# FFN gate and up products by Strassen's scheme for two of eight k-pairs, in a float32 kernel of split matmuls

## The chip, the cores and the metric

One core of a Trainium2 chip. The metric is the device time of one execution in microseconds; the kernel before was run three times. TensorE is the matmul engine, VectorE (DVE) and ScalarE (ACT) do elementwise work, GpSimd (POOL) and SyncE (SP) issue DMAs here.

## What is computed

Two layers on x of 256 tokens by 2048, all in float32. The first is a hybrid attention layer, the second a FFN, a mixer and another FFN. The change touches the two FFNs alone:

```python
def rmsnorm(x, g): ...
def swiglu(x, w_gate, w_up, w_down):
    return (jax.nn.silu(x @ w_gate) * (x @ w_up)) @ w_down
```

x is 256 x 2048, w_gate and w_up are 2048 x 5632, w_down is 5632 x 2048. The result is added, times 0.5, to the residual.

## The kernel before, in words

**Split products.** TensorE works on fp32r operands. To keep float32 accuracy each operand is split into a rounded part and the rest: weights into whi and wlo, activations into act_hi and act_lo. A product is three matmuls: hi x whi, lo x whi, hi x wlo. The fourth is left out.

**Groups and units.** Weights stream from HBM in groups of TILES = 2 blocks of 128 rows (a k-pair) by W = 512 columns, 512 KB. A ring of RING = 4 places holds raw, whi and wlo. Of each group SyncE loads raw (`load`, L388; waits until wlo of the group four before is done, lo_ready), ScalarE rounds it to whi (`split_hi`, L1036; waits for the load and for group_used of the group four before), VectorE subtracts to get wlo (`split_lo`, L1496), and TensorE does 2 tiles x 2 token halves x 3 = 12 matmuls of 128x128 by 512 (`groups`, L573; all of one tile kind before the next, so wlo is waited for just before the last four). ScalarE and VectorE run AHEAD = 3 groups ahead of TensorE. A unit is all k-pairs (G_D = 8) of one block of 512 columns and fills one PSUM pair acc (two token halves).

**The FFN loop.** For each of FF_CHUNKS = 11 column blocks there is a gate unit and an up unit. The first block is written out, the other 10 are turns of a hardware loop (`at.loop`) on each engine; `ffn` in TensorE's, ScalarE's, VectorE's and SyncE's programs (L917, L2090, L407). At the end of the gate unit ScalarE puts the silu of acc times the row scale in g_sb (`activate`, L1171). At the end of the up unit VectorE forms h_sb (`gated`, L2114: two scalar_tensor_tensor from PSUM, then a transpose of 32x32 squares into h_turned). GpSimd then exchanges the squares through DRAM (`exchange`, L482: one DMA out, a wait, four DMAs back into h_back), and in the next turn at j == 5 ScalarE (`turned_hi`, L1114) and VectorE (`turned_lo`, L1570) write h_hi and h_lo from h_back. Each engine works strictly in the order written, so whatever stands behind these waits for them.

**Semaphores.** `Place` (L154) counts groups, units and so on, and turns the counts into targets of waits inside loops. `raw_in` has one semaphore for each ring place, `lo_ready`, `hi_ready` and `group_used` count groups, `acc_free` the halves of a PSUM pair that were read. The PSUM banks tr0, tr1, s_ps and o_ps are used in attention and not in the FFN loop.

Of the kernel before, what the change touches and what calls it, by code (L numbers as in the profile page):

```python
# [24 lines left out]
F32 = mybir.dt.float32  # L25
F32R = mybir.dt.float32r
I32 = mybir.dt.int32
ACT = mybir.ActivationFunctionType
# [4 lines left out]
P = 128  # L33
D = 2048
SEQ = 256
# [55 lines left out]
ALL_GROUPS = (FIRST_GROUPS + CHUNKS * G_D + 2 * (FF_CHUNKS * 2 * G_D + CHUNKS * KF // TILES)  # L91
              + 15 * G_D + CHUNKS * (2 * G_D + 2 + 6) + CHUNKS * G_D)

# [57 lines left out]
    return n  # L151


class Place:  # L154

    def __init__(self):
        self.n = dict(group=0, unit=0, job=0, chunk=0, ready=0, score=0, value=0, turn=0)  # L160
        self.turn, self.adds = None, {}

    def target(self, what, more=0, times=1, ring=1):
# [19 lines left out]
def build(nc, x, positions, w_in, w_uq, w_ukv, b_forget, w_out, g_post, ffn1_w_gate_2, ffn1_w_up_2,  # L183
# [3 lines left out]
    with ctx:  # L187
# [80 lines left out]
        h_turned, h_back = top, top + QUADS * TURN * 4  # L268
        h_turned, _ = place_at("h_turned", [P, CHUNK], F32, h_turned)
        h_back, _ = place_at("h_back", [P, CHUNK], F32, h_back)  # L270
        gfinal, top = place_at("gfinal", [P, D], F32, top)


        sg_hi, top = place_at("sg_hi", [P, SG_GROUPS, SEQ], F32R, region)
# [94 lines left out]
        vector_step = sem("vector_step")  # L369
        pool_step = sem("pool_step")  # L370
        out_a, out_v, out_sent = sem("out_a"), sem("out_v"), sem("out_sent")

        block = ctx.enter_context(nc.Block())


        after_first = FIRST_GROUPS + CHUNKS * G_D
        after_ffn1 = after_first + FF_CHUNKS * 2 * G_D + CHUNKS * KF // TILES
# [7 lines left out]
        def _(sp):  # L385
# [19 lines left out]
                at.n["unit"] += 1  # L405

            def ffn(w_gate, w_up, w_down):  # L407
                for i in at.loop(sp, FF_CHUNKS, dict(group=2 * G_D, unit=2)):
                    unit(w_gate, G_D, i * W)
                    unit(w_up, G_D, i * W)  # L410
                for c in range(CHUNKS):
                    unit(w_down, KF // TILES, c * W)

# [155 lines left out]
        def _(pe):  # L569
# [3 lines left out]
            def groups(count, hi, lo, width=W, opening_from=None, between=None, ends_by_half=0):  # L573
# [73 lines left out]
                at.n["unit"] += 1  # L647

            def job(blocks):

# [266 lines left out]
            def ffn(first_one):  # L917
                chunks_split[0] = at.n["chunk"]

                def second_half():  # L920

                    pe.wait_ge(post_part, 2)
                    for part in range(2):
                        transpose_part(1, part)
                    at.n["chunk"] += 1
                    at.n["ready"] += 1
                    keep_warm(2)

                for j in groups(G_D, act_hi, act_lo, opening_from=POST_OPENED if first_one else None,
                                between=second_half):  # L930
                    if first_one:
                        if j in (0, 2, 4):
                            opening(j // 2 + 1)
                    if not first_one and j == 3:
                        exchanged()
                        chunk_is_split()
                        transpose_chunk(xres, 3 * W)
                    if not first_one and j == 5:
                        chunk_is_split()
                for j in groups(G_D, act_hi, act_lo):  # L940
                    pass
                for i in at.loop(pe, FF_CHUNKS - 1, dict(group=2 * G_D, unit=2, chunk=1)):
                    for j in groups(G_D, act_hi, act_lo):
                        if j == 3:
                            h_turns()
                    for j in groups(G_D, act_hi, act_lo):
                        pass
# [83 lines left out]
        def _(act):  # L1031
# [4 lines left out]
            def split_hi(n):  # L1036
# [10 lines left out]
                if m >= RING:  # L1047

                    act.wait_ge(group_used, at.target("group", n + 1 - RING))
                nc.scalar.activation(whi[:, slot, :, 0:width], raw[:, slot, :, 0:width],  # L1050
                                     ACT.Copy).then_inc(hi_ready, 1)

            def groups(count, last_split=True):
                for j in range(count):
                    if last_split or j < count - 1:
                        split_hi(AHEAD)
                    at.n["group"] += 1
                    yield j
                at.n["unit"] += 1

            def unit_ready():

# [278 lines left out]
            def ffn(norm, first_one):  # L1341
# [12 lines left out]
                        norm_ready(norm)  # L1354
                        activate(g_sb, ACT.Silu, norm)
                for j in groups(G_D):
                    pass
                at.n["turn"] = EX_FFN1 if first_one else EX_FFN2
                for i in at.loop(act, FF_CHUNKS - 1, dict(group=2 * G_D, unit=2, chunk=1, turn=1)):
                    for j in groups(G_D):  # L1360
                        if j == 5:
                            turned_hi(h_hi, i * 4, h_back[:])
                        if j == 7:
                            activate(g_sb, ACT.Silu, norm)
                    for j in groups(G_D):
                        pass
# [119 lines left out]
        def _(dve):  # L1486
# [9 lines left out]
            def split_lo(n):  # L1496

                m = at.n["group"] + n
                if at.turn is None and m >= ALL_GROUPS:
                    return  # L1500
                width = LAT2 if LAT2_FIRST <= m < LAT2_END else W
                slot = m % RING
                dve.wait_ge(hi_ready, at.target("group", n + 1))
                nc.vector.tensor_tensor(wlo[:, slot, :, 0:width], raw[:, slot, :, 0:width],  # L1504
                                        whi[:, slot, :, 0:width].bitcast(F32), ALU.subtract).then_inc(lo_ready, 1)

            def groups(count, last_split=True):
                for j in range(count):
# [581 lines left out]
            def ffn(norm, first_one):  # L2090
# [23 lines left out]
                def gated():  # L2114
# [6 lines left out]
                    for half in range(HALVES):  # L2121
# [5 lines left out]
                                        h_sb[:].rearrange("p h (k q j) -> p (h k) q j", q=QUADS, j=QUAD)  # L2127
                                        ).then_inc(turned, 1)

                for j in groups(G_D):  # L2130
                    if j == 7:
                        gated()
                at.n["turn"] = EX_FFN1 if first_one else EX_FFN2
                for i in at.loop(dve, FF_CHUNKS - 1, dict(group=2 * G_D, unit=2, chunk=1, chunk_job=2, turn=1)):
                    for j in groups(G_D):
                        if j == 5:
                            turned_lo(h_hi, h_lo, i * 4, h_back[:])
                    for j in groups(G_D):
                        if j == 7:
                            gated()  # L2140
# [284 lines left out]
```

## Time and profile before

| what | value |
|---|---|
| device time, three runs | 2606.83, 2606.23, 2605.05 us; median 2606.23 |
| profiled execution: span, first to last instruction | 2603.4 us |
| its own time | not listed apart; one of the runs above, 1.7 to 3.4 us over the span |
| TensorE, matmuls | busy 2594.2 us, 11669 matmuls |
| VectorE | busy 1503.5 us (58%) |
| ScalarE | busy 1191.6 us (46%) |
| mean DMA rate | 216 GB/s |

The span is what the trace covers. Busy matmul time counts overlapping matmuls once; the mean of one matmul (391 ns) includes its overlap with its neighbours, so the spacing of matmuls is read from the timeline.

### The profile page before, as it was taken

The numbers are of one execution on the slowest core, as the hardware profiler recorded it, in microseconds if no ns is written. First come the engines' busy times: TensorE is split into PE (matmuls) and PEld (weight loads), VectorE is DVE, ScalarE is ACT, GpSimd is POOL, SyncE is SP. The second block draws the span as 40 slices with busy tenths as digits, with TensorE's granted clock in tenths as the row PEclk, the third lists the DMA queues.
The fourth block names the chain that finished last, engine by engine and source line by source line (L and its number), as shares of the span: only waits on it lengthen the run. The fifth ranks groups of instructions, "written<-read, shape, count | busy, mean of one in ns | idle before, by whom it ended". The sixth has DMA issues, their size and how long they took to land.

```text
span 2603.4 us, 31908 instructions
## 1 busy us (share of the span) xinstructions
PE 2594.2 (100%) x11669; PEld 2154.1 (83%) x11669; DVE 1503.5 (58%) x1725; ACT 1191.6 (46%) x1362; POOL 204.5 (8%) x345
## 2 busy tenths in 40 slices
PE   9999999999999999999999999999999999999998
PEld 8888888888888888888888888888888888888887
DVE  7766665755555555556555765555655555555554
ACT  5544554544444444444444644444454444444333
POOL 0122110000000000001100420000000000000000
PEclk9999999999999999999999999999999999999999
DMA  7787785677777766668876677665777777777564
GB/s 217 255 255 233 217 242 182 206 209 225 209 225 209 226 209 209 210 210 258 241 216 193 199 224 216 210 209 193 236 209 217 217 216 217 214 219 228 193 194 157
DMA packets 280065, 561.51 MB, mean 216 GB/s; under 512 B 22826, under 2 KB 25784, under 8 KB 279720
## 3 DMA queue, kind: packets, MB, share of 16 engines
q1 hardware_dynamic: 257120, 489.61, 62.0%
q0 software_dynamic: 22208, 70.19, 9.1%
q8 instruction: 56, 0.92, 0.1%
q10 hardware_dynamic: 648, 0.52, 0.1%
q14 instruction: 33, 0.27, 0.0%
HBM read 526.02 MB, written 34.22 MB: 215 GB/s over the span
## 4 chain that ended last, share of the span: by engine, by line
PE 99%; DMA 0%; ACT 0%; SPq 0%; issue 0%; DVE 0%; ACTq 0%
PE acc L586 97%; PE s_ps L740 1%; PE o_ps L764 1%; PE tr L656 1%; DMA xres<-in_x 0%; PE tr L991 0%; ACT xres L1477 0%; ACT g_sb L1145 0%; ACT act_hi L1094 0%; DVE xres L1782 0%; SPq L396 0%; SPq L417 0%; SPq L415 0%; ACT root L1152 0%; PE s_ps L869 0%
## 5 line engine op out<-in xcount | busy, mean ns | idle before, releaser
L1504 DVE TENSOR_TENSOR wlo<-raw,whi 128x1024 fp32r<-128x1024 f32 x929 | 1130.5, 1224 | 982.0 <-ACT whi L1050 977.2
L1050 ACT ACTIVATE whi<-raw 128x1024 fp32r<-128x1024 f32 x929 | 977.8, 1057 | 1148.7 <-PE acc L586 1115.2
L586 PE MATMUL acc<-whi,act_hi 128*128 128x512 f32 (+1 forms) x2560 | 690.5, 391 | 0.1
L586 PE MATMUL acc<-whi,act_lo 128*128 128x512 f32 (+1 forms) x2560 | 683.3, 388 | 0.0
L586 PE MATMUL acc<-wlo,act_hi 128*128 128x512 f32 (+1 forms) x2560 | 683.1, 388 | 0.0
L586 PEld LDWEIGHTS acc<-whi,act_lo 128*128 128x128 f32 x2560 | 479.4, 188 | 100.2 <-DVEq L1545 0.4
L586 PEld LDWEIGHTS acc<-wlo,act_hi 128*128 128x128 f32 x2560 | 479.5, 188 | 99.9 <-DVE wlo L1504 0.3
L586 PEld LDWEIGHTS acc<-whi,act_hi 128*128 128x128 f32 x2560 | 474.9, 188 | 94.8 <-issue 0.3
L586 PE MATMUL acc<-whi,h_hi 128*128 128x512 f32 x704 | 188.8, 389 | 0.0
L586 PE MATMUL acc<-wlo,h_hi 128*128 128x512 f32 x704 | 188.8, 389 | 0.0
L586 PE MATMUL acc<-whi,h_lo 128*128 128x512 f32 x704 | 188.8, 389 | 0.0
L586 PEld LDWEIGHTS acc<-whi,h_lo 128*128 128x128 f32 x704 | 132.1, 188 | 27.5
L586 PEld LDWEIGHTS acc<-wlo,h_hi 128*128 128x128 f32 x704 | 132.1, 188 | 27.4
L586 PEld LDWEIGHTS acc<-whi,h_hi 128*128 128x128 f32 x704 | 132.1, 188 | 27.4
L485 POOL DMA_DIRECT2D turn_dram<-h_turned x25 | 14.0, 561 | 1110.4 <-DVE h_turned L2126 947.5
L499 POOL DMA_DIRECT2D h_back<-turn_dram x100 | 54.7, 554 | 76.4 <-DMA turn_dram<-h_turned 73.7
L1176 ACT ACTIVATE g_sb<-acc,rs 128x512 f32<-128x512 f32 x44 | 27.9, 686 | 33.2 <-PE acc L586 33.2
L1194 ACT ACTIVATE lat<-lat,soft 128x128 f32<-128x128 f32 (+1 forms) x32 | 14.3, 448 | 61.8 <-DVE soft L1734 61.8
L2122 DVE SCALAR_TENSOR_TENSOR h_sb<-acc,rs,g_sb 128x512 f32<-128x512 f32 x44 | 31.0, 746 | 12.0 <-PE acc L586 12.0
L586 PE MATMUL acc<-whi,o_hi 128*128 128x512 f32 x128 | 35.3, 392 | 0.0
L586 PE MATMUL acc<-whi,o_lo 128*128 128x512 f32 x128 | 34.9, 389 | 0.0
L586 PE MATMUL acc<-wlo,o_hi 128*128 128x512 f32 x128 | 34.9, 389 | 0.0
(281 smaller groups left out, 1372.8 us busy)
## 6 DMA issues: line engine op xcount, KB each, us to landing
raw<-in_w_in SPq DMA_DIRECT2D x280, 512.0 KB, 4.5
raw<-in_ffn_w_gate SPq DMA_DIRECT2D x176, 512.0 KB, 4.4
raw<-in_ffn_w_up SPq DMA_DIRECT2D x176, 512.0 KB, 4.1
raw<-in_ffn_w_down SPq DMA_DIRECT2D x176, 512.0 KB, 4.6
raw<-in_w_out SPq DMA_DIRECT2D x64, 512.0 KB, 4.7
turn_dram<-h_turned POOLq DMA_DIRECT2D x25, 512.0 KB, 3.2
h_back<-turn_dram POOLq DMA_DIRECT2D x100, 128.0 KB, 5.6
raw<-in_w_sg_out SPq DMA_DIRECT2D x24, 512.0 KB, 4.2
```

The lines of the kernel that those rows point to most:

```text
L485: pool.dma_start(turn_dram[n % 2][:, :, 0:run], left.rearrange("p (q r) -> p q r", q=QUADS)).then_inc(turn_left, 16)
L499: pool.dma_start(back[quad * QUAD:(quad + 1) * QUAD].rearrange("p (a r) -> p a r", a=QUADS), blocks[n % 2][quad][:, :, 0:run]).then_inc(tu ...
L586: return nc.tensor.matmul(pair[:, half, 0:width], left[:, j * TILES + t, half * P:(half + 1) * P], right[:, (first_group + j) % RING, t, 0 ...
L656: last = nc.tensor.transpose(tr[bank][0:rows, cols], src, ident[0:src.shape[0], 0:src.shape[0]])
L740: last = nc.tensor.matmul(out_cols, left, right, start=(n == 0), stop=(n == len(terms) - 1), skip_group_check=True)
L764: last = nc.tensor.matmul(o_ps[:, qb * P:(qb + 1) * P], left, right, start=(n == 0), stop=(n == len(terms) - 1), skip_group_check=True)
L1050: nc.scalar.activation(whi[:, slot, :, 0:width], raw[:, slot, :, 0:width], ACT.Copy).then_inc(hi_ready, 1)
L1176: last = nc.scalar.activation(dest[:, half, :], a[:, half, :], func, scale=scaled(norm, half))
L1194: last = nc.scalar.activation(src_of[qb], src_of[qb], ACT.Exp, bias=soft[:, 1, qb:qb + 1], scale=scale, accum_out=soft[:, 2, qb:qb + 1])
L1504: nc.vector.tensor_tensor(wlo[:, slot, :, 0:width], raw[:, slot, :, 0:width], whi[:, slot, :, 0:width].bitcast(F32), ALU.subtract).then_in ...
L2122: last = nc.vector.scalar_tensor_tensor(h_sb[:, half, :], a[:, half, :], scaled(norm, half), g_sb[:, half, :], ALU.mult, ALU.mult)
```

## The change

In the 10 loop turns of each FFN, gate and up are computed together in 20 groups. k-pairs 2 to 7 are done as before, gate ("left") and up ("right"). k-pairs 0 and 1 are each a product of 2x2 blocks: token halves by two k tiles, times two k tiles by gate and up. Strassen's scheme gives its four results from seven block products in place of eight, each still three matmuls. Such a k-pair takes four groups. "four_left" is the loaded gate tiles, "four_right" the loaded up tiles (only the second is split and multiplied), "outer" and "inner" are sums of weight tiles, which VectorE writes into the next two ring places of raw (`outer_sums`, `inner_sums`) and which are then split like loaded ones. The four sums of activations are formed once for each FFN (`combine_activations`) in the first block's up unit, and rounded by ScalarE. The extra products go to the four free banks; VectorE recombines them (`fours_out`) at group 13 and adds acc at the end of the turn (`paired_gated`). The silu runs on g_sb in SBUF after that. SyncE's first block is now written out too. Cut to its core:

```diff
+FOURS = 2
+CHUNK_ORDER = ([("left", k) for k in range(2, 6)] + four(0) + [("left", 6), ("left", 7)] + four(1)
+               + [("right", k) for k in range(2, G_D)])
+q1, q5, q6, q7 = s_ps, o_ps, tr[0], tr[1]
...
 SyncE, ffn
-                for i in at.loop(sp, FF_CHUNKS, dict(group=2 * G_D, unit=2)):
+                unit(w_gate, G_D, 0)
+                unit(w_up, G_D, 0)
+                for i in at.loop(sp, FF_CHUNKS - 1, dict(group=CHUNK_GROUPS, unit=2)):
+                    for kind, k in CHUNK_ORDER:
+                        if kind in ("left", "four_left"):
+                            load(w_gate, k, i * W + W)
+                        elif kind in ("right", "four_right"):
+                            load(w_up, k, i * W + W)
+                        else:
+                            at.n["group"] += 1
...
 TensorE, paired: what each kind of group multiplies (bank, left hi, left lo, tile)
+                    if kind == "four_left":
+                        return [block(q1[:], 0, 2 * k, 0), block(left[:, 0, :], 0, 2 * k + 1, 1)]
+                    if kind == "four_right":
+                        return [combined(right[:, 0, :], k, 0, 1)]
+                    if kind == "outer":
+                        t1 = outer_tiles(m - 2)[1]
+                        return [combined(q5[:], k, 1, t1), combined(q7[:], k, 3, 1 - t1)]
+                    return [combined(q6[:], k, 2, 0), block(left[:, 1, :], 1, 2 * k + 1, 1)]
...
 ScalarE, loop turn
+                    for j in paired():
                         if j == 5:
                             turned_hi(h_hi, i * 4, h_back[:])
+                        if j == LAST_FOUR:
+                            unit_ready()
+                            nc.scalar.activation(g_sb[:, 0, :], q1[:], ACT.Copy).then_inc(q1_copied, 1)
+                        if j == LAST_FOUR + 2:
+                            act.wait_ge(acc_free[at.n["unit"] % 2], at.target("unit", 0, 2, 2) + 2)
...
 VectorE, split_lo and the sums
+                if sums_next:
+                    outer_sums(m + 1)
                 dve.wait_ge(hi_ready, at.target("group", n + 1))
...
+                if sums_next:
+                    inner_sums(m + 1)
+            def outer_sums(m):
+                raw_filled(m)
+                raw_filled(m + 1)
+                dve.wait_ge(lo_ready, at.target("group", m - 1 - at.n["group"]))
+                slot = (m + 2) % RING
+                nc.vector.tensor_tensor(raw[:, slot, :, :], raw_blocks[:, outer_tiles(m)[0], :],
+                                        raw[:, (m + 1) % RING, 0, :].unsqueeze(1).to_broadcast([P, TILES, W]),
+                                        ALU.add).then_inc(raw_in[slot], 16)
+            def inner_sums(m):
+                raw_filled(m + 2)
+                dve.wait_ge(lo_ready, at.target("group", m - at.n["group"]))
+                slot = (m + 3) % RING
+                nc.vector.tensor_tensor(raw[:, slot, 0, :], raw[:, (m + 2) % RING, outer_tiles(m)[1], :],
+                                        raw[:, (m + 1) % RING, 1, :], ALU.add).then_inc(sum_step, 1)
+                dve.wait_ge(sum_step, at.target("sums"))
+                nc.vector.tensor_tensor(raw[:, slot, 1, :], raw[:, slot, 0, :], raw[:, m % RING, 1, :],
+                                        ALU.add).then_inc(raw_in[slot], 16)
+            def fours_out():
+                unit_ready()
+                dve.wait_ge(q1_copied, at.target("paired", 1))
+                sum_settled(nc.vector.tensor_tensor(h_sb[:, 1, :], q6[:], g_sb[:, 0, :], ALU.add))
+                sum_settled(nc.vector.tensor_tensor(g_sb[:, 1, :], q7[:], h_sb[:, 1, :], ALU.add))
+                sum_settled(nc.vector.tensor_tensor(h_sb[:, 0, :], q5[:], h_sb[:, 1, :], ALU.subtract))
+                sum_settled(nc.vector.tensor_tensor(h_sb[:, 1, :], q5[:], g_sb[:, 1, :], ALU.subtract))
+                dve.sem_inc(q_free, 1)
+                nc.vector.tensor_tensor(g_sb[:], acc[at.n["unit"] % 2][:], g_sb[:],
+                                        ALU.add).then_inc(acc_free[at.n["unit"] % 2], 2)
...
 VectorE, end of a turn
+                def paired_gated():
+                    unit_ready()
+                    right = (at.n["unit"] + 1) % 2
+                    for half in range(HALVES):
+                        nc.vector.tensor_tensor(h_sb[:, half, :], acc[right][:, half, :], h_sb[:, half, :],
+                                                ALU.add).then_inc(acc_free[right], 1)
+                    dve.wait_ge(acc_free[right], at.target("unit", 1, 2, 2) + 2)
+                    dve.wait_ge(gate_ready, at.target("paired", 1))
...
+                        if j == LAST_FOUR:
+                            fours_out()
+                        if j == CHUNK_GROUPS - 1:
+                            paired_gated()
```

`LAST_FOUR` is 13. `outer_tiles` picks the two tiles of gate and up that an outer sum adds to. `combine_activations` is one sum of 1024 columns, four of 256, a wait for ScalarE's rounding, and one difference; it runs at j == 1, the rounding at j == 2.

## Rows read from the trace of the kernel before

**Rows 1.** The page: engine totals, granted clock by slices, chain that ended last.
```profile
PE 2594.2 (100%) x11669; PEld 2154.1 (83%) x11669; DVE 1503.5 (58%) x1725; ACT 1191.6 (46%) x1362; POOL 204.5 (8%) x345
...
PEclk9999999999999999999999999999999999999999
...
PE 99%; DMA 0%; ACT 0%; SPq 0%; issue 0%; DVE 0%; ACTq 0%
```
**Rows 2.** Busy time by engine, 506.9 to 942 us; waits there: total, times, longest.
```profile
core 0: us, PE busy (x) PEld busy (x) DVE busy (x) ACT busy (x) POOL busy (x), PEclk, DMA share, GB/s
506.90:942.00 435.10, 435.10 (x1921) 360.29 (x1920) 232.93 (x211) 192.01 (x200) 27.51 (x50) 1.00 0.73 217
...
ACT whi L1050 <- PE acc L586: 222.0, 145, 1.7
DVE wlo L1504 <- ACT whi L1050: 194.2, 135, 2.6
```
**Rows 3.** Timeline of a turn: start, duration, engine, line; in brackets idle before.
```profile
894.20 1.07 PE L586 MATMUL acc<-whi,act_hi 128*128 128x512 f32 x4
894.55 1.41 DVE L2122 SCALAR_TENSOR_TENSOR h_sb<-acc,rs,g_sb 128x512 f32<-128x512 f32 x2 [0.56 <-PE acc L586]
896.00 1.25 DVE L2126 STREAM_TRANSPOSE h_turned<-h_sb 128x1024 f32<-128x1024 f32 x1
897.16 2.32 DVE L1504 TENSOR_TENSOR wlo<-raw,whi 128x1024 fp32r<-128x1024 f32 x2
899.63 1.07 PE L586 MATMUL acc<-whi,act_hi 128*128 128x512 f32 x4
899.84 1.06 ACT L1050 ACTIVATE whi<-raw 128x1024 fp32r<-128x1024 f32 x1 [1.66 <-PE acc L586]
900.93 1.23 DVE L1504 TENSOR_TENSOR wlo<-raw,whi 128x1024 fp32r<-128x1024 f32 x1 [1.45 <-ACT whi L1050]
901.01 2.19 POOL L499 DMA_DIRECT2D h_back<-turn_dram  x4 [2.91 <-DMA turn_dram<-h_turned]
902.36 1.07 PE L586 MATMUL acc<-whi,act_hi 128*128 128x512 f32 x4
...
909.96 1.16 ACT L1122 ACTIVATE h_hi<-h_back 128x512 f32 x2 [0.90 <-DMA h_back<-turn_dram]
...
938.07 1.41 DVE L2122 SCALAR_TENSOR_TENSOR h_sb<-acc,rs,g_sb 128x512 f32<-128x512 f32 x2 [0.56 <-PE acc L586]
```
**Rows 4.** Timeline of TensorE at the kernel's end, twelve matmuls running to one bank.
```profile
2585.14 0.62 PE L586 MATMUL acc<-whi,h_hi 128*128 128x512 f32 x2
...
2587.86 0.62 PE L586 MATMUL acc<-whi,h_hi 128*128 128x512 f32 x2
```
**Rows 5.** Groups of instructions by form: count, busy us, mean ns, idle before.
```profile
L2087 DVE TENSOR_TENSOR xres<-xres,gfinal 128x512 f32<-128x512 f32 x6 | 3.9, 688 | 0.2
L2321 DVE TENSOR_TENSOR ln_gb<-ln_gb 128x1024 f32<-128x1024 f32 x4 | 4.9, 1225 | 0.1
L1581 DVE TENSOR_TENSOR h_lo<-h_back,h_hi 128x512 f32 x40 | 25.8, 687 | 6.7 <-ACT h_hi L1122 6.6
L1122 ACT ACTIVATE h_hi<-h_back 128x512 f32 x40 | 23.0, 623 | 13.5 <-DMA h_back<-turn_dram 13.5
L1176 ACT ACTIVATE g_sb<-acc,rs 128x512 f32<-128x512 f32 x44 | 27.9, 686 | 33.2 <-PE acc L586 33.2
```
**Rows 6.** DMA issues, six successive 2.72 us stretches from 899.07; us to landing.
```profile
raw<-in_ffn_w_up SPq DMA_DIRECT2D x1, 512.0 KB, 6.3
raw<-in_ffn_w_up SPq DMA_DIRECT2D x1, 512.0 KB, 7.0
raw<-in_ffn_w_up SPq DMA_DIRECT2D x1, 512.0 KB, 5.9
raw<-in_ffn_w_up SPq DMA_DIRECT2D x1, 512.0 KB, 4.4
raw<-in_ffn_w_up SPq DMA_DIRECT2D x1, 512.0 KB, 3.5
raw<-in_ffn_w_up SPq DMA_DIRECT2D x1, 512.0 KB, 3.6
```
**Rows 7.** Timeline of GpSimd in the second FFN, one exchange's way back.
```profile
2059.22 1.10 POOL L499 DMA_DIRECT2D h_back<-turn_dram  x2 [3.17 <-DMA turn_dram<-h_turned]
2062.82 1.10 POOL L499 DMA_DIRECT2D h_back<-turn_dram  x2 [2.51 <-issue]
```
**Rows 8.** The tile raw: who waited for its loads (us, times).
```profile
  ACT whi L1050: 32.2, 19
```

More of the change, by code:

```diff
@@ L151, in raw_target, with outer_tiles @@
     return n
+def outer_tiles(m):
+    left, right = m % RING, (m + 1) % RING
+    blocks = (TILES * left, TILES * right + 1)
+    if blocks[0] < blocks[1]:
+        return slice(blocks[0], blocks[1] + 1, blocks[1] - blocks[0]), 0
+    return slice(blocks[1], blocks[0] + 1, blocks[0] - blocks[1]), 1
 class Place:
     def __init__(self):
-        self.n = dict(group=0, unit=0, job=0, chunk=0, ready=0, score=0, value=0, turn=0)
+        self.n = dict(group=0, unit=0, job=0, chunk=0, ready=0, score=0, value=0, turn=0, paired=0, sums=0)
         self.turn, self.adds = None, {}
@@ L270, in build @@
         h_back, _ = place_at("h_back", [P, CHUNK], F32, h_back)
+        four_hi, four_lo = (h[:, KF - 4 * FOURS // TILES:KF, :].rearrange("p k n -> p (k n)").rearrange(
+            "p (q i n) -> p q i n", q=FOURS, i=4) for h in (h_hi, h_lo))
         gfinal, top = place_at("gfinal", [P, D], F32, top)
+        four_raw = h_turned[:].rearrange("p (q i n) -> p q i n", q=FOURS, i=4)
+        four_x = h_sb[:].rearrange("p h n -> p (h n)").rearrange("p (k n) -> p k n", n=SEQ)
         sg_hi, top = place_at("sg_hi", [P, SG_GROUPS, SEQ], F32R, region)
@@ L941, in ffn @@
                     pass
-                for i in at.loop(pe, FF_CHUNKS - 1, dict(group=2 * G_D, unit=2, chunk=1)):
-                    for j in groups(G_D, act_hi, act_lo):
+                pe.wait_ge(four_ready, 1 if first_one else 2)
+                for i in at.loop(pe, FF_CHUNKS - 1, dict(group=CHUNK_GROUPS, unit=2, chunk=1, paired=1)):
+                    for j in paired(act_hi, act_lo):
                         if j == 3:
                             h_turns()
-                    for j in groups(G_D, act_hi, act_lo):
-                        pass
                 for c in range(CHUNKS):
@@ L1049, in split_hi @@
                     act.wait_ge(group_used, at.target("group", n + 1 - RING))
-                nc.scalar.activation(whi[:, slot, :, 0:width], raw[:, slot, :, 0:width],
+                tiles = slice(1, 2) if KIND.get(m) == "four_right" else slice(0, TILES)
+                nc.scalar.activation(whi[:, slot, tiles, 0:width], raw[:, slot, tiles, 0:width],
                                      ACT.Copy).then_inc(hi_ready, 1)
@@ L1059, in groups, with paired @@
                 at.n["unit"] += 1
+            def paired():
+                for j in range(CHUNK_GROUPS):
+                    split_hi(AHEAD)
+                    at.n["group"] += 1
+                    yield j
+                at.n["unit"] += 2
+                at.n["paired"] += 1
             def unit_ready():
@@ L1502, in split_lo @@
                 slot = m % RING
+                sums_next = KIND.get(m + 1) == "four_left"
+                if sums_next:
+                    outer_sums(m + 1)
+                tiles = slice(1, 2) if KIND.get(m) == "four_right" else slice(0, TILES)
                 dve.wait_ge(hi_ready, at.target("group", n + 1))
-                nc.vector.tensor_tensor(wlo[:, slot, :, 0:width], raw[:, slot, :, 0:width],
-                                        whi[:, slot, :, 0:width].bitcast(F32), ALU.subtract).then_inc(lo_ready, 1)
+                nc.vector.tensor_tensor(wlo[:, slot, tiles, 0:width], raw[:, slot, tiles, 0:width],
+                                        whi[:, slot, tiles, 0:width].bitcast(F32), ALU.subtract).then_inc(lo_ready, 1)
@@ new lines, in split_lo, with raw_filled @@
+                if sums_next:
+                    inner_sums(m + 1)
+            raw_blocks = raw[:].rearrange("p s t n -> p (s t) n")
+            def raw_filled(m):
+                target = raw_target(m)
+                if at.turn is not None:
+                    target = target + at.turn * (16 * at.adds["group"] // RING)
+                dve.wait_ge(raw_in[m % RING], target)
+            def outer_sums(m):
[6 more added lines that the diff above has]
+                                        ALU.add).then_inc(raw_in[slot], 16)
@@ L2133, in ffn @@
                 at.n["turn"] = EX_FFN1 if first_one else EX_FFN2
-                for i in at.loop(dve, FF_CHUNKS - 1, dict(group=2 * G_D, unit=2, chunk=1, chunk_job=2, turn=1)):
-                    for j in groups(G_D):
+                for i in at.loop(dve, FF_CHUNKS - 1, dict(group=CHUNK_GROUPS, unit=2, chunk=1, chunk_job=2, turn=1,
+                                                          paired=1, sums=SUMS_PER_CHUNK)):
+                    for j in paired():
                         if j == 5:
                             turned_lo(h_hi, h_lo, i * 4, h_back[:])
-                    for j in groups(G_D):
-                        if j == 7:
-                            gated()
+                        if j == LAST_FOUR:
+                            fours_out()
+                        if j == CHUNK_GROUPS - 1:
+                            paired_gated()
                 next_gain = GAINS["mix"]
```

124 lines of the change are left out of this document (111 added, 13 removed).

## The prediction

> **What bounds the kernel now.** I read the page's engine totals first [rows 1]: TensorE is busy for all of the span and holds 99% of the chain that ended last, at a granted clock of 0.9 or more in every slice. Then one stretch with ten turns of the FFN loop [rows 2]: TensorE has no gap, at clock 1.00, while VectorE is busy for 233 of 435 us and ScalarE for 192. The waits [rows 2] show both standing before a split of the next weights until matmuls are done: 222 us of ScalarE for TensorE, 194 us of VectorE for ScalarE. So the time is the number of matmuls times their spacing, as long as nobody is late. The timeline [rows 3] gives the spacing: twelve matmuls of a group start at 899.63, the next twelve at 902.36, 2.72 us, or 0.2267 us each; the turn is 43.52 us (gated product at 894.55 and at 938.07) for 192 matmuls.
>
> **What a group costs its feeders.** By the same rows, whi starts 0.21 us after TensorE has left the group four places back and takes 1.06; wlo follows 0.03 later and takes 1.23; then its slot of raw is reloaded. The lead is three groups of 2.72 us, and wlo is wanted only for the last third of its own group. That lead hides everything now.
>
> **What goes.** Two k-pairs of each turn need 2 x 21 matmuls, not 2 x 24: 186 per turn, and 6 x 0.2267 = 1.36 us less. Over 2 x 10 turns that is 27.2 us. The order of the banks differs (four_right sends three matmuls running to one bank); at the kernel's end twelve matmuls to one bank take 2587.86 - 2585.14 = 2.72 us [rows 4], so this costs nothing. If nothing were late: 2606.2 - 27.2 = 2579.
>
> **What comes.** In a turn of 20 groups (0 to 19; time 0 is TensorE's start of group 0) the fours are 4 to 7 and 10 to 13. TensorE needs 4.76 us for a four, where four ring places used to last 10.88, and two of the four places hold sums that VectorE writes. Durations [rows 5]: a sum of 1024 columns 1.23, of 512 0.69, a copy of 512 from PSUM 0.69, turned halves on ScalarE 1.15 for two. Two VectorE instructions with no wait between them take 2.32, so the second starts 0.10 before the first ends [rows 3]; one that waits for its predecessor I put 0.03 after it, like wlo after whi. The Trainium skill (VectorE: DVE Perf Modes, section "The DRAIN you can't avoid") says that the next instruction starts only when the pipe has emptied and that leaving out semaphores saves nothing; rows 3 disagree by that 0.10, and by the page the sum below would be some 16 us higher, 2657.
>
> I follow one turn (E3 is the end of group 3; undisturbed ends 10.88, 12.24, 12.92, 14.28, 15.64, then 18.36 and so on).
> (a) VectorE, end of the turn before. The product is formed at 0.36, as now (894.55 - 894.20 [rows 3]), but it first adds acc to the recombined halves (two of 512, 1.30), then multiplies (1.41) and turns (1.25): ready at 4.38, not 3.05, so the exchange leaves 1.33 later. Then sum outer(4) to 5.51, wlo 3 to 6.64, the two inner sums to 8.08, wlo 4 to 9.21, wlo 5 to 9.80, wlo 6 to 10.93. All are in time for TensorE. whi 7 waits for E3: 10.88 + 0.21 + 1.06 = 12.15, so wlo 7 ends at 13.41.
> (b) SyncE loads 8, 9, 10, 11 behind wlo 4, 5, 6, 7: issued at 9.38, 9.97, 11.10, 13.58, no longer 2.72 apart. They fall on the exchange's way back, issued from about 8.1 on (4.38 + 901.01 - 897.25). Loads issued beside that now land after 6.3, 7.0, 5.9 and 4.4 us, later ones after 3.5 to 3.6 [rows 6]. By their distance from it I take 6.3, 6.2, 5.6, 4.6 (estimates between these rows): landed 15.68, 16.17, 16.70, 18.18. Bounds: 3.6 each, and 7.0, 7.0, 6.3, 5.4.
> (c) whi 8 ends at 16.79, TensorE starts 8 at 16.82, not 15.64: **1.18 lost**. h_back lands 12.7 after the turning (909.96 - 897.25 [rows 3]), at 17.1; ScalarE, which has whi 9 queued behind turned_hi, ends the latter at 18.2 and whi 9 at 19.3, VectorE ends h_lo at 18.9. TensorE is at 8 until 19.54.
> (d) Behind h_lo VectorE does outer(10), which needs load 11, to 20.3, wlo 9 to 21.47 (wanted 21.35, **0.15 lost**), the inner sums to 22.9, wlo 10 to 24.04 (TensorE at 10 from 22.41, wants it at 23.3: **0.76 lost**). wlo 11 to 13 are in time; E13 = 27.92.
> (e) Load 14 goes only behind wlo 10: 24.2 + 3.6 = 27.8, whi 14 ends 28.92, **1.03 lost** before group 14.
> (f) fours_out at group 13 (q1 copy, four sums with waits, one of 1024: 4.9 us) delays wlo 17 to 37.6, wanted at 38.9; nothing lost. The silu on SBUF is on nobody's way; with fours_out gone later by over 1.3 us group 17 would wait.
> Sum: 3.1 lost - 1.36 gained = **+1.75 us a turn**, a turn of 45.27; times 20, +35.0. Against this execution's span 2603.4 that is 2638.4, and on the median shown, which is 2.8 above the span: **2641**.
> Hidden: combining activations once per FFN (VectorE about 5 us, ScalarE 1.06) in the second unit of the first turn, where wlo 5 slips to about 4.8 us after E1 and is wanted at 10; its cover is that unit's idle VectorE, and without it the price were under 10 us in all. Peeling SyncE's first turn, zero. The later exchange before the down projection meets groups of 2.72 with a lead of over 7 us at that place, zero; ends: 0 and the 1.33 of its delay, twice.
>
> **Rivals.**
> 1. *The lead hides it all.* For it: feeders half idle now [rows 2]. Against: their idleness is spread over 2.72 us groups, and (d) and (e) have two loads in series. 2579. Chance 0.08.
> 2. *The loads land undisturbed.* With no load in flight between groups 0 and 4 the exchange may come back about 1 us earlier and all loads take 3.6: then (c) goes, (d) and (e) stay in part; the turn is 44.05, +11. In the best corner, the exchange never waited for, 43.39: -3. So 2617, and down to 2603. Chance 0.22. It turns to a gain only if outer(10) runs before 17.2 and group 14 loses under 1.36 in sum.
> 3. *Forecast*, chance 0.46.
> 4. *Worse contention.* Loads at their upper bounds, exchange back after 13.4, load 14 after 4.4: turn 46.77, +65, 2671. For it: loads now go in bunches, and one exchange already had its four reads split by 2.51 us of standing [rows 7]. Chance 0.20.
> 5. *The clock falls.* For 14 of 20 turns or so one 12-matmul group at half clock (2.72 more) would give +38 on top, about 2680. Against: [rows 1] show no lower slice, and my gaps are near 1 us. The Trainium skill (TensorE: Matmul & The Clock Gate, section "HAM oscillation — how this bites in real kernels") says that a TensorE waiting for data between short bursts can be throttled each time; no row here shows it. Chance 0.04.
> That the change would not remove matmuls is excluded by the diff: 21 for 24 is written out.
>
> **How the numbers follow.** 0.2%, about what a measurement of this kernel can tell, is 5.2 us. Faster: rival 1 and the best corner of 2 (0.05): 0.13. Same: a part of 2 (0.07). Slower: the rest of 2 (0.10), 3, 4, 5: 0.80. The range leaves out rival 1, most of 5 and the tail of 4: 2600 to 2674.
>
> **What would show it.** In the profile of after: MATMUL counts lower by 120; turns of 45.3 us between turnings; ScalarE's whi waiting for DMA raw in about two places a turn (now 19 times in the whole kernel [rows 8]); TensorE gaps of about 1 us before groups 8 and 14, each 20 times, and before the wlo products of group 10; h_back landing near 17 us after the turn's start with ScalarE behind it. It is wrong if TensorE keeps no gap, if gaps stand at group 4 or 17 instead (VectorE's own work), or if loads 8 to 11 land in under 4 us.

## The result, and the profile after

The changed kernel takes **2670.24 us** (median of 4 runs, 2666.60 to 2673.38) against 2606.53 us before (4 runs beside it, 2605.05 to 2610.46): ratio 1.0244, 95% interval 1.0229 to 1.0258, so 63.7 us slower. The sign and the range of the forecast hold; its size, +35, does not. The profiled execution of after is the fastest of the four: own time 2666.6 us, span 2664.8, mean granted clock 0.996 (before 0.999). Its span is 61.4 us longer than the 2603.4 of the profiled execution of before.

Totals and chain on the page of after, to be held against [rows 1]:
```profile
span 2664.8 us, 32709 instructions
PE 2597.6 (97%) x11549; PEld 2132.5 (80%) x11549; DVE 1769.4 (66%) x2077; ACT 1259.4 (47%) x1464; POOL 202.7 (8%) x345
PE 54%; issue 22%; DMA 11%; DVE 9%; ACT 2%; POOL 1%; DVEq 0%; ACTq 0%; SPq 0%; POOLq 0%
raw<-in_ffn_w_gate SPq DMA_DIRECT2D x176, 512.0 KB, 5.2
raw<-in_ffn_w_up SPq DMA_DIRECT2D x176, 512.0 KB, 4.6
h_back<-turn_dram POOLq DMA_DIRECT2D x100, 128.0 KB, 2.9
```
TensorE held 99% of the chain; now it holds 54%, DMA has 11% and VectorE 9%, and 22% is "issue", time in which the profile shows nothing that the engine waited for. TensorE is idle for 67 us (2664.8 - 2597.6), 57 of them in the two stretches of gate and up. Who waited there (total us, times, longest):
```profile
ACT whi L1164 <- DMA raw<-in_ffn_w_gate: 156.8, 83, 4.7
ACT whi L1164 <- DMA raw<-in_ffn_w_up: 92.6, 70, 3.8
PE acc L747 <- ACT whi L1164: 44.4, 38, 4.6
PE s_ps L754 <- DVE wlo L1637: 9.2, 15, 0.6
PE acc L754 <- DVE wlo L1637: 3.2, 13, 0.4
ACT h_hi L1244 <- DMA h_back<-turn_dram: 15.0, 3, 5.5
```
ScalarE waited 19 times for a load of raw in the whole kernel before [rows 8]; now 153 times for loads of gate and up alone. One turn (group 0 starts at 733.36), timeline of after: start, duration, engine, line, in brackets the idle before. It answers to [rows 3].
```profile
733.77 1.22 DVE L1637 TENSOR_TENSOR wlo<-raw,whi 128x1024 fp32r<-128x1024 f32 x1 [1.22 <-ACT whi L1164]
734.92 1.28 DVE L2346 TENSOR_TENSOR h_sb<-acc,h_sb 128x512 f32<-128x512 f32 x2
737.68 1.25 DVE L2354 STREAM_TRANSPOSE h_turned<-h_sb 128x1024 f32<-128x1024 f32 x1
...
742.39 2.19 POOL L548 DMA_DIRECT2D h_back<-turn_dram  x4 [2.61 <-DMA turn_dram<-h_turned]
742.68 4.09 DVE L1637 TENSOR_TENSOR wlo<-raw,whi 128x1024 fp32r<-128x1024 f32 x4
744.07 2.11 SPq L437 DMA_DIRECT2D raw<-in_ffn_w_gate  x3
...
749.58 1.06 ACT L1164 ACTIVATE whi<-raw 128x1024 fp32r<-128x1024 f32 x1 [4.08 <-DMA raw<-in_ffn_w_gate]
750.55 1.14 ACT L1244 ACTIVATE h_hi<-h_back 128x512 f32 x2
750.69 1.20 PE L747 MATMUL acc<-whi,act_hi 128*128 128x512 f32 x4 [1.53 <-ACT whi L1164]
751.81 1.29 DVE L1792 TENSOR_TENSOR h_lo<-h_back,h_hi 128x512 f32 x2
753.33 1.23 DVE L1657 TENSOR_TENSOR raw<-raw 128x1024 f32<-128x1024 f32 x1 [0.23 <-issue]
755.75 1.20 PE L754 MATMUL acc<-wlo,act_hi 128*128 128x512 f32 x4 [0.22 <-DVE wlo L1637]
758.47 0.50 PE L754 MATMUL s_ps<-wlo,act_hi 128*128 128x512 f32 x1 [0.61 <-DVE wlo L1637]
762.04 1.06 ACT L1164 ACTIVATE whi<-raw 128x1024 fp32r<-128x1024 f32 x1 [3.59 <-DMA raw<-in_ffn_w_up]
763.15 1.20 PE L747 MATMUL acc<-whi,act_hi 128*128 128x512 f32 x4 [0.53 <-ACT whi L1164]
...
783.63 1.25 DVE L2354 STREAM_TRANSPOSE h_turned<-h_sb 128x1024 f32<-128x1024 f32 x1
```
TensorE waits in four places: before group 8 (750.69) for a whi that had waited 4.08 us for load 8; at the wlo products of 9 (755.75) and of 10 (758.47) for VectorE, whose outer sum (753.33) stood behind h_lo until 753.10 and then another 0.23 us for load 11, issued at 746.80 and landed 6.4 us later; and before group 14 (763.15) for a whi that had waited 3.59 us for load 14. The same turn by stretches (stretch, us, busy PE, PEld, DVE, ACT, POOL, then clock, share of the DMA engines, GB/s):
```profile
737.68:747.50 9.82, 9.82 (x45) 8.14 (x44) 8.88 (x9) 2.76 (x3) 2.75 (x5) 1.00 0.44 141
747.50:752.50 5.00, 3.47 (x16) 2.55 (x15) 1.83 (x3) 2.92 (x4) 0.00 (x0) 1.00 0.94 347
752.50:758.50 6.00, 5.17 (x23) 3.62 (x21) 5.57 (x8) 3.72 (x5) 0.00 (x0) 1.00 0.01 3
758.50:772.00 13.50, 12.97 (x56) 10.43 (x57) 10.87 (x12) 6.15 (x7) 0.00 (x0) 1.00 0.81 272
772.00:783.63 11.63, 11.63 (x53) 9.64 (x52) 9.19 (x10) 7.01 (x8) 0.00 (x0) 1.00 0.68 225
```
**Loads come in bunches.** During a four two of the four places of raw hold sums, so SyncE has nothing to load; then all places come free nearly at once. SyncE issues nothing between 732.58 and 744.07. Before, the stretch of ten turns moved 217 GB/s [rows 2], and in one turn of it (720 to 760) pieces of 5 and 10 us moved 144 to 256; now 347 GB/s and a DMA share of 0.94 are followed by 3 GB/s and 0.01. Loads 8 to 11 land after 5.4, 6.1, 6.2 and 6.4 us, in the bunch and beside the exchange.

**The sum closes.** Turns are 46.47 us long on average in the first FFN ((970.56 - 505.87)/10 between turnings) and 47.06 in the second ((2423.06 - 1952.49)/10), before 43.52. Against the undisturbed 42.16 (186 x 0.2267), ten turns of each lose 43.1 + 49.0 = 92.1 us; less the 27.2 that went, that is +64.9 in the loops. The span of this execution grew by 61.4, so the sum closes within 3.5 us, and the rest of the program is that much shorter, most of it (3.2 us) behind the last turning. The 63.7 is the difference of the medians, not of these two executions.

### The profile page after: what moved, and what is told of

It reads as the page before. It is cut to its first block, busy times and chain, and to the rows that moved or that the text cites. A ratio compares the mean times of both kernels' runs of the same rounds, so it can differ in the third digit from the quotient of the medians.

```text
span 2664.8 us, 32709 instructions
## 1 busy us (share of the span) xinstructions
PE 2597.6 (97%) x11549; PEld 2132.5 (80%) x11549; DVE 1769.4 (66%) x2077; ACT 1259.4 (47%) x1464; POOL 202.7 (8%) x345
## 4 chain that ended last, share of the span: by engine, by line
PE 54%; issue 22%; DMA 11%; DVE 9%; ACT 2%; POOL 1%; DVEq 0%; ACTq 0%; SPq 0%; POOLq 0%
PE acc L635 45%; DMA raw<-in_ffn_w_up 7%; DVE wlo L1637 6%; PE acc L747 2%; PE acc L754 2%; PE acc L750 2%; DMA raw<-in_ffn_w_gate 2%; ACT whi L1164 2%; DMA qk<-turn_dram 1%; DMA turn_dram<-turned_s 1%; DVE raw L1667 1%; PE s_ps L854 1%; DVE raw L1657 1%; PE tr L770 1%; DMA turn_dram<-mix_turned 1%
## 5 line engine op out<-in xcount | busy, mean ns | idle before, releaser
L1637 DVE TENSOR_TENSOR wlo<-raw,whi 128x1024 fp32r<-128x1024 f32 (+2 forms) x1009 | 1191.9, 1200 | 763.4 <-ACT whi L1164 756.2
L1164 ACT ACTIVATE whi<-raw 128x1024 fp32r<-128x1024 f32 (+2 forms) x1009 | 1037.4, 1038 | 1113.9 <-PE acc L635 641.2
L635 PE MATMUL acc<-whi,act_hi 128*128 128x512 f32 (+1 forms) x1280 | 348.5, 393 | 0.1
L635 PE MATMUL acc<-whi,act_lo 128*128 128x512 f32 (+1 forms) x1280 | 341.2, 388 | 0.0
L635 PE MATMUL acc<-wlo,act_hi 128*128 128x512 f32 (+1 forms) x1280 | 341.1, 388 | 0.0
L747 PE MATMUL acc<-whi,act_hi 128*128 128x512 f32 x1040 | 294.1, 395 | 44.4 <-ACT whi L1164 44.4
L754 PE MATMUL acc<-wlo,act_hi 128*128 128x512 f32 x1040 | 293.2, 395 | 3.3 <-DVE wlo L1637 3.2
L750 PE MATMUL acc<-whi,act_lo 128*128 128x512 f32 x1040 | 292.3, 394 | 0.0
L635 PEld LDWEIGHTS acc<-wlo,act_hi 128*128 128x128 f32 x1280 | 239.3, 188 | 50.1 <-DVE wlo L1637 0.4
L747 PEld LDWEIGHTS acc<-whi,act_hi 128*128 128x128 f32 x1040 | 192.8, 188 | 99.3 <-ACT whi L1164 60.7
L635 PEld LDWEIGHTS acc<-whi,act_hi 128*128 128x128 f32 x1280 | 234.7, 188 | 44.9 <-issue 0.3
L754 PEld LDWEIGHTS acc<-wlo,act_hi 128*128 128x128 f32 x1040 | 196.2, 190 | 50.7 <-DVE wlo L1637 10.5
```

The costliest lines, as they stand in the source:

```text
L635: return nc.tensor.matmul(pair[:, half, 0:width], left[:, j * TILES + t, half * P:(half + 1) * P], right[:, (first_group + j) % RING, t, 0 ...
L747: nc.tensor.matmul(bank, left_hi, whi[:, slot, t, :], start=fresh, stop=False, skip_group_check=True)
L750: nc.tensor.matmul(bank, left_lo, whi[:, slot, t, :], start=False, stop=False, skip_group_check=True)
L754: last = nc.tensor.matmul(bank, left_hi, wlo[:, slot, t, :], start=False, stop=uses[str(bank)] == o and t == TILES - 1, skip_group_check=True)
L1164: nc.scalar.activation(whi[:, slot, tiles, 0:width], raw[:, slot, tiles, 0:width], ACT.Copy).then_inc(hi_ready, 1)
L1637: nc.vector.tensor_tensor(wlo[:, slot, tiles, 0:width], raw[:, slot, tiles, 0:width], whi[:, slot, tiles, 0:width].bitcast(F32), ALU.subtr ...
```

## The experiments

Every kernel ran beside the kernel before on its chip (2606.2 to 2607.1 us there). Five of them (sums of 16 columns, half loads, both, no recombination, small exchange) leave part of the work out and return other numbers, so they price a part and are no versions to use; the others do all of it. The question: is the loss VectorE's sums, the loads, the recombination, the exchange, or their order?

**Sums of 16 columns.** All instructions, waits and signals stay; the weight sums write only 16 columns.
```diff
-nc.vector.tensor_tensor(raw[:, slot, :, :], raw_blocks[:, outer_tiles(m)[0], :], ...
+nc.vector.tensor_tensor(raw[:, slot, :, 0:16], raw_blocks[:, outer_tiles(m)[0], 0:16], ...
```


> The three weight sums of each four write 16 columns instead of 512 (the rest of those two ring places keeps old data, so the products are of other numbers); all waits stay. Theory A (VectorE's sums stand between the loads that landed and the splits that release the next loads, so the second four runs two loads in series behind them): without 3.7 us of sums per turn of groups 3 to 14 the waits at wlo 9, wlo 10 and before group 14 go and loads 8 to 11 are issued over 2 us earlier; turns near 42.8 us, 2590 to 2602 us in all. Theory B (the loads themselves, bunched because two of four ring places hold sums and slowed by each other, set the time): the bunch only moves, a wait of 1 us or more stays before group 8 or 10, and the time stays above 2630 us.

Measured 2617.79 us (2616.29 to 2619.75), ratio 1.0044 (1.0027 to 1.0061), 52 less than after, and still 39 above the 2579 at which TensorE never waits. What is left, in the waits of this kernel:
```profile
ACT whi L1164 <- DMA raw<-in_ffn_w_up: 83.9, 80, 3.4
ACT whi L1164 <- DMA raw<-in_ffn_w_gate: 79.1, 70, 4.1
```
The result lies between the two theories: without the sums' time, ScalarE still waits 163 us for loads.

**Half loads.** Gate and up loads in the loop bring 256 of 512 columns; all work on them stays.
```diff
+if part is not None:
+    main, cols = part, bass.ds(col, part)
...
-load(w_gate, k, i * W + W)
+load(w_gate, k, i * W + W, part=W // 2)
...
-load(w_up, k, i * W + W)
+load(w_up, k, i * W + W, part=W // 2)
```


> The gate and up loads of the loop turns bring 256 of 512 columns (the rest keeps old data); VectorE, ScalarE and TensorE do the same work. Theory B: landings fall from over 5 us to about 3, the waits before groups 8 and 14 fall by 2 us each turn, time 2610 to 2630 us. Theory A with landings as in the rows of before: the chain of VectorE stays, each of the two loads in series gets at most 1 us shorter, 2635 to 2655 us.

Measured 2590.10 us (2588.62 to 2590.95), ratio 0.9936 (0.9920 to 0.9953), 80 less than after and 20 under the least that either theory gave. Loads (KB, us to landing) and the one wait for sums' work that TensorE keeps:
```profile
raw<-in_ffn_w_gate SPq DMA_DIRECT2D x160, 256.0 KB, 3.2
raw<-in_ffn_w_up SPq DMA_DIRECT2D x160, 256.0 KB, 2.9
PE s_ps L756 <- DVE wlo L1639: 2.8, 10, 0.6
```
With all sums in full, landing 2 us earlier is nearly enough. So loads and sums aren't two losses beside each other but one chain, in which time taken out anywhere counts: 52 + 80 is more than the 91 there is.

**Both.** The two diffs together.

> Sums of 16 columns and loads of 256 columns together (data of other numbers): neither VectorE's sums nor the landings press. The floor of 186 matmuls per turn: 2606.5 less 27.2, 2578 to 2582 us. A time over 2586 would mean that the ring of four places itself costs a short four something, whatever fills it.

Measured 2577.97 us (2577.59 to 2578.59), ratio 0.9888 (0.9871 to 0.9905): the floor. Turnings are 758.73 - 716.57 = 42.16 us apart, 186 x 0.2267 to the hundredth. The matmuls' 27 us are real, and the new order of places and banks costs nothing by itself.

**No recombination.** The four sums of fours_out write 16 columns (the sum with acc stays whole).
```diff
-sum_settled(nc.vector.tensor_tensor(h_sb[:, 1, :], q6[:], g_sb[:, 0, :], ALU.add))
+sum_settled(nc.vector.tensor_tensor(h_sb[:, 1, 0:16], q6[:, 0:16], g_sb[:, 0, 0:16], ALU.add))
```


> The four recombining sums at group 13 work on 16 columns instead of 512 (so h is of other numbers), the sum of 1024 columns stays. Theory C (they hold back wlo 17 and with it the loads of the next turn, so that its wlo 2, the end of turn on VectorE and load 8 come 1.2 us late): the product is formed 0.4 us after the turn's start and not 1.6, the wait before group 8 shrinks from 1.7 to 0.5 us, 20 to 25 us less in all, 2645 to 2652. The prediction's step (f) (nothing lost): 2668 to 2672.

Measured 2645.55 us (2643.45 to 2647.01), ratio 1.0150 (1.0133 to 1.0167), 24.7 less than after. This contradicts step (f) of the prediction. In after fours_out (767.25 to 771.50) holds back the splits, four loads again go out close together and land after 3.5, 4.6, 5.4 and 5.5 us, and wlo 2 of the next turn ends late; the product behind it is formed 1.56 us after that turn's start. Here it is formed 0.20 after it (729.27 against 729.07), and TensorE's gap before group 8, in the same turn, is 0.27 us in place of 1.53.

**Small exchange.** All but the first exchange of each FFN move 16 of 256 columns a run, each way; h_back is otherwise stale.
```diff
+pool.dma_start(turn_dram[n % 2][:, :, 0:16],
+               h_turned[:].rearrange("p (q r) -> p q r", q=QUADS)[:, :, 0:16]).then_inc(turn_left, 16)
```


> From the second block of columns of each FFN on, the exchange moves 16 of 256 columns of each run (the rest of h_back is old data); its DMAs, waits and order stay. If the exchange's way back is what makes load 8 land after 5.4 us (it is issued 1.7 us before that load), the landing falls to about 4.2 and the wait before group 8 from 1.7 to about 0.5 us: 2645 to 2653 us. If the four loads of the bunch slow each other alone, the exchange is harmless and nothing changes: 2665 to 2673.

Measured 2648.43 us (2645.10 to 2650.69), ratio 1.0160 (1.0143 to 1.0177), 21.8 less than after, in the expected range. Its exchange and TensorE's waits:
```profile
h_back<-turn_dram POOLq DMA_DIRECT2D x80, 8.0 KB, 1.9
PE acc L759 <- ACT whi L1176: 17.3, 24, 1.1
PE acc L766 <- DVE wlo L1649: 14.0, 21, 1.1
```
The waits for whi fall from 44.4 to 17.3 us, but part of it only moves on to wlo 9 (14.0): earlier loads meet the same VectorE.

**Turned halves later.** h_back is split at group 9, not 5.
```diff
-                        if j == 5:
+                        if j == 9:
                             turned_hi(h_hi, i * 4, h_back[:])
```


> ScalarE and VectorE take h_back at group 9 of the turn instead of 5. The prediction's steps (c) and (d) put h_hi and h_lo ahead of whi 9 and outer(10); if they are on the path, 0.3 to 0.6 us less per turn, 2655 to 2664 us. If outer(10) waits for load 11 in any case (the profile of after has h_lo ending 0.2 us before that sum starts), nothing: 2666 to 2673.

Measured 2660.22 us (2655.58 to 2661.17), ratio 1.0201 (1.0184 to 1.0218), 10.0 less than after and in the first expected range. But its trace doesn't show that h_lo ahead of outer(10) was what held it. Without h_lo before it, the outer sum waits for load 11 itself (a row of its timeline, one of its waits):
```profile
753.01 1.23 DVE L1657 TENSOR_TENSOR raw<-raw 128x1024 f32<-128x1024 f32 x1 [1.46 <-DMA raw<-in_ffn_w_up]
PE acc L747 <- ACT whi L1164: 24.3, 24, 2.0
```
The gain is in the waits for whi, 24.3 us in all in place of 44.4, in the turn shown 0.94 us before group 8 in place of 1.53. Part of it is lost again in a new wait for wlo of 6.7 us (19 times) in the second four, where the splits of h_back now stand. Why the wait before group 8 shrank was not tried apart.

**The fours further apart.** Three groups between them, not two, and the second four among the up groups.
```diff
-CHUNK_ORDER = ([("left", k) for k in range(2, 6)] + four(0) + [("left", 6), ("left", 7)] + four(1)
-               + [("right", k) for k in range(2, G_D)])
+CHUNK_ORDER = ([("left", k) for k in range(2, 7)] + four(0) + [("left", 7), ("right", 2), ("right", 3)]
+               + four(1) + [("right", k) for k in range(4, G_D)])
```


> Same work, other order: gate pairs 2 to 6, four(0) at groups 5 to 8, gate 7, up 2 and 3, four(1) at 12 to 15, up 4 to 7. With bursts of loads and VectorE's chain together as the cause, one group more ahead of the first four and one more between them take away most of the waits at wlo 9 and 10 and part of the others, but both bursts remain and four(1)'s recombination now ends nearer to the turn's end: 43.0 to 45.0 us per turn, 2596 to 2636 us, middle 2616. If only the number of fours counts and not their distance, 2660 or more.

Measured 2626.29 us (2624.15 to 2627.30), ratio 1.0075 (1.0058 to 1.0092), 43.9 less than after. Nothing was left out: of the 91 us lost, nearly half was the order.

**This order, and h_back at group 10.** The diff above and `j == 10` in place of `j == 5`.

> The spaced order with h_back taken at group 10 instead of 5, so both edits that helped alone. Additive: 2626 less 6 to 10 us, 2616 to 2620. If with the spaced order load 12 and not h_back is what outer waits for: 2624 to 2628.

Measured 2620.86 us (2616.86 to 2622.27), ratio 1.0055 (1.0036 to 1.0073), the best of the complete versions with two fours, and still slower than before. It is 5.4 less than the spaced order alone, just past the additive range (2616 to 2620). TensorE hardly waits for whi any more (17.7 us in the spaced order), and its longest waits are those for wlo inside the fours:
```profile
PE o_ps L754 <- DVE wlo L1637: 11.9, 20, 0.6
PE s_ps L754 <- DVE wlo L1637: 7.7, 15, 0.6
```

**Evenly spread.** The second four at groups 14 to 17 of 20, h_back at 10 (`j == 10` as above).
```diff
+CHUNK_ORDER = ([("left", k) for k in range(2, 6)] + four(0) + [("left", 6), ("left", 7)]
+               + [("right", k) for k in range(2, 6)] + four(1) + [("right", 6), ("right", 7)])
```


> Two fours as far apart as the turn allows: four(0) at groups 4 to 7, gate 6 and 7, up 2 to 5, four(1) at 14 to 17, up 6 and 7; h_back is taken at group 10. Each burst of loads has six whole groups behind it to be made good. If distance is what counts, less is lost than in the spaced order (about 1.9 us per turn): 2600 to 2620 us. Against it: the recombination now starts two groups before the turn's end, and the product and the next turn's sums queue behind it; if that decides, the wait before group 8 is 2 us or more and the time 2630 or more.

Measured 2699.19 us (2698.53 to 2700.92), ratio 1.0354 (1.0336 to 1.0372), the slowest of all. Waits and timeline of this kernel:
```profile
PE acc L747 <- DVE g_sb L1715: 53.8, 18, 3.6
PE acc L747 <- ACT whi L1164: 14.9, 20, 2.7
```
```profile
693.25 2.07 PE L747 MATMUL acc<-whi,act_hi 128*128 128x512 f32 x4 [3.14 <-DVE g_sb L1715]
...
696.61 1.07 PE L754 MATMUL acc<-wlo,act_hi 128*128 128x512 f32 x4
```
The expectation had a late recombination, but not this wait: fours_out alone gives acc of gate back, and with the last four at group 17 the next turn's group 0 waits for it some 3 us, 18 times. At 15 of the 18 the matmuls behind the gap run at half clock (2.07 us for four, not 1.07), and the mean clock is 0.987. The waits for whi did fall, from 44.4 to 14.9 us, but a gap of 3 us in each turn gives the feeders time too, so this run doesn't show that the spreading did it.

**One four.** One of eight k-pairs in place of two, at groups 7 to 10 of 18; two column blocks to a loop turn. Nothing is left out.
```diff
-FOURS = 2
+FOURS = 1
+BLOCKS = 2
...
-CHUNK_ORDER = ([("left", k) for k in range(2, 6)] + four(0) + [("left", 6), ("left", 7)] + four(1)
-               + [("right", k) for k in range(2, G_D)])
+CHUNK_ORDER = ([("left", k) for k in range(1, G_D)] + four(0)
+               + [("right", k) for k in range(1, G_D)])
...
-for i in at.loop(pe, FF_CHUNKS - 1, dict(group=CHUNK_GROUPS, unit=2, chunk=1, paired=1)):
+for i in at.loop(pe, (FF_CHUNKS - 1) // BLOCKS,
+                 dict(group=CHUNK_GROUPS * BLOCKS, unit=2 * BLOCKS, chunk=BLOCKS, paired=BLOCKS)):
+    for b in range(BLOCKS):
```


> One k-pair of eight by seven products instead of two, placed at groups 7 to 10 of 18, after all of gate; the loop takes two blocks of columns per turn so that the ring's places stay fixed. TensorE's work is 13.6 us under before. Theory A and B alike: one four alone is covered by the lead of three groups, since nothing else has to be fed within the next 10 us and the exchange is back before; waits under 0.2 us per block, 2593 to 2598 us, faster than before by 0.3 to 0.5%. If a single four also stalls (about 1.2 us before the group behind it), 2612 to 2620 us.

Measured **2592.20 us** (2591.81 to 2592.91), ratio 0.9943 (0.9926 to 0.9959): 14.9 faster than before and the only complete version here that beats it. Its page (span and totals), and one of its waits:
```profile
span 2591.1 us, 32344 instructions
PE 2580.7 (100%) x11609; PEld 2143.4 (83%) x11609; DVE 1689.2 (65%) x1977; ACT 1234.9 (48%) x1424; POOL 204.9 (8%) x345
```
```profile
DVE raw L1664 <- DMA raw<-in_ffn_w_up: 90.8, 20, 5.3
```
Two turnings in its timeline are at 634.24 and 677.08, so a block takes 42.84 us, which is 189 x 0.2267: it is at its own floor, 2606.2 - 20 x 3 x 0.2267 = 2593. VectorE still waits 4.5 us a block for the four's last load (90.8 in 20), and it costs nothing: seven groups of 2.72 us stand on either side of the four, time for the feeders to get their lead back before the next one. That the blocks are two to a loop turn (18 groups are no multiple of the ring's four places, 36 are) was not tried apart from this.

## Why the prediction was right or wrong

**Right: what bounds it and what goes.** 120 matmuls fewer (11549), [rows 4] held, and the kernel with both reductions reaches the predicted 2579 to 1 us. Rival 1, that the lead hides all, is the kernel with half loads and small sums, not this one.

**Right: the places.** In the turn shown (45.95 us, one of the shorter ones) TensorE lost, before group 8, at 9, at 10 and before 14, 1.68, 0.39, 0.77 and 0.69 us; the steps had 1.18, 0.15, 0.76 and 1.03. Together 3.53 against 3.12. That loads 8 to 11 would land after some 6 us, and that load 14 is in series behind wlo 10, is in the trace as written. So rival 2 falls: the loads did not land undisturbed.

**Wrong: step (f), "nothing lost".** I followed fours_out up to wlo 17 and stopped. Its delay also bunches the loads of the next turn's first groups, so that step (a) begins late: the product is formed 1.56 us after the start in place of 0.36, load 8 goes at 10.71 in place of 9.38. Without the recombination 24.7 us go. The steps counted the turn as if it started with all feeders three groups ahead, and did not run a second turn to see whether it does.

**Wrong: part of step (c).** In the turn shown the four reads of the exchange landed after 2.8, 2.9, 2.7 and 4.9 us (median over the program 2.9, before 5.6), while the places held by sums kept the loads away and the kernel moved 141 GB/s. h_back was there 15.6 us after the turn's start, not 17.1, before whi 8 was done, and was waited for 3 times in all. What the exchange cost was its share of the landings of loads 8 to 11, 21.8 us by the small exchange, and 10.0 that taking h_back later gave back, though not by way of outer(10) as (d) had it.

**Wrong: landings 8 to 11 as a falling row.** (b) had 6.3, 6.2, 5.6, 4.6; measured 5.4, 6.1, 6.2, 6.4. I took them by their distance from the exchange; in a bunch the last one waits for the others as well. With the small exchange the same four landed after 3.7, 4.5, 5.1 and 5.3 us (medians over the first FFN's ten turns), so the rising row is the bunch, and the exchange adds most to the first. The last one is what outer(10) needs. Load 14 by contrast was less late than in (e).

**Mis-sized: two things I had only as rivals.** Rival 5, in small: after gaps of about 2 us (4.63 in one) the matmuls came at half clock, in five stretches of the loops. Timeline of after, and one window at that place (columns as above, the clock third from the end):
```profile
658.00 1.67 PE L747 MATMUL acc<-whi,act_hi 128*128 128x512 f32 x4 [1.98 <-ACT whi L1164]
...
661.17 1.43 PE L754 MATMUL acc<-wlo,act_hi 128*128 128x512 f32 x4
```
```profile
658.60:659.60 1.00, 1.00 (x4) 0.80 (x3) 1.00 (x2) 1.00 (x2) 0.00 (x0) 0.50 0.85 330
```
A clock of 0.50 is 1.2 GHz, of 1.00 is 2.4. The mean clock went from 0.999 to 0.996, 0.003 of 2665 us, which at half clock is 16 us long and costs 8 (an estimate; the five stretches together are 17 us). And rival 4's mechanism, an exchange whose reads are split by standing, came in one turn, of 49.4 us:
```profile
2098.27 1.10 POOL L548 DMA_DIRECT2D h_back<-turn_dram  x2 [2.75 <-DMA turn_dram<-h_turned]
2101.88 1.09 POOL L548 DMA_DIRECT2D h_back<-turn_dram  x2 [2.51 <-issue]
2109.94 1.15 ACT L1244 ACTIVATE h_hi<-h_back 128x512 f32 x2 [5.54 <-DMA h_back<-turn_dram]
2112.09 1.68 PE L747 MATMUL acc<-whi,act_hi 128*128 128x512 f32 x4 [4.63 <-ACT whi L1164]
```
The value is nearly rival 4's 2671, but its own case is not what happened as a rule. The loops grew by 64.9 us where the steps had 35. Of the 30 between, some 14 are the turn shown against the forecast's turn (45.95 between its turnings against 45.27, times 20) and 8 the clock; the other 8 are slower turns, this last one 3.5 us over the one shown, whose causes I did not work out one by one.

**Luck.** The measured time lies within the range, and what bounds the kernel and where it waits were foreseen. But the range reached up to it for rival 4's sake, whose mechanism came once in 20 turns; the step that counted most beyond the forecast, the recombination reaching into the next turn, was put at nothing.

**The unit prices held.** The sum used that two VectorE instructions with no wait between them overlap by 0.10 us. The four wlo from 742.68 on, three of 1.22 us and one of 512 columns of 0.68, took 4.09 us where end to end they would take 4.34: 0.08 at each joint. The prediction took "The DRAIN you can't avoid" (Trainium skill, VectorE: DVE Perf Modes) to rule this out. The section does say that the next operation doesn't start until the pipe is empty, but it adds that "A next op that is not held starts earlier", so these rows, where the next one starts 1.14 us after one of 1.22, don't contradict it, and the 2657 doesn't follow from it. Restarts were not in the sum: the first four matmuls behind a gap take 1.20 us and not 1.07, which is part of the 14 us above.

## What to carry to other kernels

If computed tiles are put into a ring that prefetches, count the places that stay free for loads: while they are short the queue has nothing to issue, and afterwards the loads come together and land in up to 1.8 times the time, so the lead is gone exactly where the next such block needs it. Follow the steps through two turns of a loop, not one, for what is late at a turn's end comes back at its start. That the held places make the bunch is read from the timeline; no run here had more places in the ring. Then try half of the change: one four per turn keeps half of the saving, all of it real, where two lose more than they save.

## What the runs showed of the hardware that I had not expected

- The same 512 KB load lands after 3.5 us when it is the first behind a pause of the loads (load 14 of the turn shown) and after 5.4 to 6.4 us in a bunch of four beside the exchange, although the kernel moves only 210 GB/s over its span, fewer than the 217 of the stretch before.
- The clock answered to gaps of 2 to 3 us in a TensorE that is over 90% busy: 1.2 GHz for the matmuls behind them, mean 0.987 with a gap of some 3 us in nearly each turn, and 0.998 to 1.000 in the other nine experiments. It did not do so each time: in after the gap of 1.91 us at 2155.91 was followed by it, those of 1.93 at 843.47 and of 1.91 at 2342.70 were not. The section "HAM oscillation — how this bites in real kernels" (Trainium skill, TensorE: Matmul & The Clock Gate) describes such a throttling for short bursts of matmuls between waits for data; before had none in its loops, and these rows show it with long bursts as well.
- GpSimd standing 2.51 us between two of four DMA issues of one exchange [rows 7] is in the profile of each of the twelve kernels, once among the exchanges of the FFNs: 2.51 us at the fourth exchange of the second FFN in eleven of them, 2.38 us at its third with the small exchange. Before, that turn took 43.52 us like the others; in after it is the one of 49.4. What it stands for the trace doesn't say, and no run here tried it.
